# A mixture-of-experts kernel on one core: the first expert weight in two transfers of 4 MB instead of four of 2 MB

## What is computed

```python
def moe_ffn(x, w_router, b_router, w_e1, b_e1, w_e2, b_e2):
    logits = (xt @ w_router + b_router).astype(jnp.float32)
    top_val, top_idx = lax.top_k(logits, TOP_K)      # TOP_K = 4
    gate = jax.nn.softmax(top_val, axis=-1).astype(x.dtype)
    ...
    def expert_block(args):
        xb, e = args
        hb = xb @ w_e1[e] + b_e1[e]
        return clamped_swiglu(hb) @ w_e2[e] + b_e2[e]
```

## Time and profile before

| | us |
|---|---|
| median of 3 runs (1545.33 to 1546.18) | 1546.01 |
| the profiled execution, its own time | 1544.39 |
| its span, first to last instruction | 1542.6 |
| expert loop, about | 600 to 1500 |

### The profile page before, as it was taken

One profiled execution on the slowest core, in us unless ns is written; L12 is line 12 of the kernel. 1 busy time (PEld: TensorE's weight loads), 2 busy tenths in 40 slices (PEclk: granted clock), 3 DMA queues, 4 the chain that ended last, 5 costly groups with the idle time before them and its releaser, 6 DMA issues.

```text
span 1542.6 us, 29979 instructions
## 1 busy us (share of the span) xinstructions
PE 1410.8 (91%) x12414; PEld 715.5 (46%) x12415; DVE 679.6 (44%) x1216; ACT 154.0 (10%) x287; POOL 328.1 (21%) x389
## 2 busy tenths in 40 slices
PE   7999999999999998999986788898789899999987
PEld 6887444458874644443332223333233334444442
DVE  5177344333334764354344334443444334434455
ACT  4112322111110120000000000000000000000001
POOL 1060000000000044233323322332233222323210
PEclk9999999999999999999999999999999999999999
DMA  6533100263317599999999999999999999999997
GB/s 220 188 123 102 28 0 1 53 200 96 95 49 307 202 367 416 420 423 422 422 423 423 420 424 424 422 421 423 424 422 422 425 422 424 423 422 420 423 394 273
DMA packets 98102, 478.52 MB, mean 310 GB/s; under 512 B 14820, under 2 KB 61316, under 8 KB 72968
## 3 DMA queue, kind: packets, MB, share of 16 engines
q1 hardware_dynamic: 84064, 457.68, 73.4%
q0 software_dynamic: 12080, 16.64, 3.0%
q10 hardware_dynamic: 1912, 3.56, 0.6%
HBM read 471.17 MB, written 23.08 MB: 320 GB/s over the span
## 4 chain that ended last, share of the span: by engine, by line
PE 70%; DMA 23%; DVE 3%; issue 2%; another core or an unknown queue 1%; ACT 1%; POOL 0%; SPq 0%; DVEq 0%; POOLq 0%; ACTq 0%
PE ps L1962 23%; DMA big<-in_w_e 22%; PE ps L2007 14%; PE ps L1655 12%; PE ps L1858 4%; PE ps L1822 4%; PE ps L1643 3%; PE ps L1739 2%; PE ps L1788 2%; PE ps L1799 2%; PE ps L1757 1%; PE ps L1806 1%; PE ps L1767 1%; DMA rest<-x_rows,P 1%
## 5 line engine op out<-in xcount | busy, mean ns | idle before, releaser
L1962 PE MATMUL ps<-big,rest 128*32 128x512 f32 x5024 | 557.9, 594 | 73.1 <-DMA big<-in_w_e 53.6
L1962 PEld LDWEIGHTS ps<-big,rest 128*32 128x32 f32 x5024 | 167.2, 110 | 448.7 <-issue 439.4
L2007 PE MATMUL ps<-big,rest 128*32 128x256 f32 x4992 | 292.0, 381 | 29.2 <-DMA big<-in_w_e 23.6
L2007 PEld LDWEIGHTS ps<-big,rest 128*32 128x32 f32 x4992 | 174.4, 110 | 154.5 <-issue 50.3
L1484 DVE MEMSET stat<- 128x1 f32 x30 | 1.8, 59 | 468.9 <-PE ps L1962 468.9
L770 POOL DMA_INDIRECT rest<-x_rows,idx x120 | 147.3, 1228 | 57.2 <-issue 31.7
L786 POOL DMA_INDIRECT expert_rows<-rest,slot x120 | 119.2, 994 | 53.9 <-issue 28.4
L1029 ACT ACTIVATE rest<-rest 128x1024 f32<-128x1024 f32 x32 | 33.9, 1060 | 898.5 <-DVE rest L1463 743.0
L778 POOL COPY idx<-P 128x4 uint32 (+1 forms) x30 | 5.5, 185 | 437.7 <-DVE rest L1485 428.6
L746 POOL IOTA P<- 128x128 f32 x1 | 0.2, 243 | 349.8 <-DVE rest L1311 349.8
L1500 DVE TENSOR_TENSOR rest<-ps,rest 128x1024 f32<-128x1024 f32 x32 | 39.2, 1225 | 66.8 <-PE ps L2007 65.8
(11 more groups left out here) (329 smaller groups left out, 1240.0 us busy)
## 6 DMA issues: line engine op xcount, KB each, us to landing
big<-in_w_e SPq DMA_DIRECT2D x187, 2048.0 KB, 24.3
rest<-in_w_in SPq DMA_DIRECT2D x14, 1024.0 KB, 5.5
big<-expert_rows SPq DMA_DIRECT2D x4, 2048.0 KB, 14.7
gate_area<-in_w_in SPq DMA_DIRECT2D x8, 512.0 KB, 4.8
rest<-in_w_in SPq DMA_DIRECT2D x8, 512.0 KB, 4.8
big<-in_w_out SPq DMA_DIRECT2D x1, 4096.0 KB, 12.8
gate_area<-in_w_e SPq DMA_DIRECT2D x2, 2048.0 KB
X<-in_x SPq DMA_DIRECT2D x4, 512.0 KB, 9.4
```

What stands on the lines that cost most here:

```text
L1962: last = mm(ps[TB * g:TB * (g + 1), h0 + b, :], rows[:, k, b, :], quarter_of(k, g), start=(k == 2 * order[0]), stop=(k == 2 * order[-1] + 1))
L2007: last = mm(ps[TB * g:TB * (g + 1), 4 + b // 2, YW * (b % 2):YW * (b % 2 + 1)], acts[:, k, b, :], rows_of(k, g), start=(first and k == 0), ...
```

## The change

`load_w1` issues two loads instead of four, each for two neighbouring pairs (32 KB in each partition, 4 MB in all), when TensorE has used the second of the two. The landing is counted on the semaphore of the odd pair. In the loop TensorE waits for it ahead of the even pair, and no longer waits ahead of the odd one. The turn that is written out ahead of the loop keeps its waits, since the pairs that it uses still come one by one.

```diff
             def load_w1(it, e):
-                for k in range(PAIRS):
+                for k in range(1, PAIRS, 2):
                     sp.wait_ge(w1_used, PAIRS * it - PAIRS + k + 1)
-                    load_pair(e, k)
+                    sp.dma_start(W1_pairs[:, k - 1:k + 1, :].rearrange("p k n -> p (k n)"), first_rows(e)[:, 4 * FF * (k - 1):4 * FF * (k + 1)]).then_inc(w1_landed[k], 16)
...
             def later_fc1(it1, blocks, pair):
 
-                if pair == SECOND_SPARE:
-                    pe.wait_ge(w1_landed[pair], 16 * it1)
-                else:
-                    pe.wait_ge(w1_landed[pair], 16 * it1 - 16)
+                if isinstance(it1, int):
+                    pe.wait_ge(w1_landed[pair], 16 * it1 if pair == SECOND_SPARE else 16 * it1 - 16)
+                elif pair % 2 == 0:
+                    pe.wait_ge(w1_landed[pair + 1], 16 * it1 - 16)
```

## The result

| | before | after |
|---|---|---|
| median of 6 runs each, us | 1546.01 | 1551.14 |
| lowest to highest, us | 1545.33 to 1546.83 | 1549.69 to 1552.64 |
| ratio, with its 95% interval | 1 | 1.0034 (1.0022 to 1.0047) |
| the profiled execution, us | 1544.39 | 1549.69 |
| its span, us | 1542.6 | 1547.9 |

The change costs 5.1 us (the ratio gives 5.3); 1549.7 was forecast. The profiled executions differ by 5.3 us, so the two traces can be compared for it.

What follows compares the result with a forecast made beforehand. The prediction took one continuous stream of about 174 loads to bound the kernel; 1.7 + 3.3 - 2.8 + 1.5 = +3.7 us on the median 1546.01 gave 1549.7, slower by 0.24%, range 1545.0 to 1555.0.

Steps and rivals of the forecast that it cites:

- (a) Fewer waits and issues: On SyncE, two waits and two loads fewer a turn; worth 0, since SyncE mostly waits for TensorE with the queue full.
- (b) Joint wait: TensorE starts two pairs together; worth 0 with two-block experts, but 5.0 us late relative to the stream from three-block experts on.
- (c) Late issue, first turn: First loop turn: the even pair's load goes out only with the odd one's; the stream loses 1.7 us (0 to 4).
- (c) Four blocks: Expert of four blocks, about 1364 to 1386 us: late joint loads make the stream lose 3.3 us (0 to 6.8).
- (d) Larger packets: All joint loads: 32 KB packets instead of 16 save 6 ns a packet; -2.8 us (0 to -2.8).
- (e) The end: Last expert: pairs 2 and 3 start at one landing, so TensorE ends later beyond the stream's loss; +1.5 us (0 to 1.6).
- The signs: DMA share below 1.01, pauses only near 622 to 635 and 1372 to 1386, first product about 5 us later, 428 to 431 GB/s.
- No cushion: In both tight places the mean engine's pause counts in full, 4 + 6.8; sum +9.5, 1555.5 us; chance 0.10.
- Packets stay at 16 KB: Rows are cut at 16 KB, so joint loads gain nothing from packet size; +6.5, 1552.5 us; chance 0.18.
- Faster: Joint loads hide all pauses behind the late engines, slowest over 5 us behind the mean; 1543.2 us; chance 0.06.
- A fixed cost per transfer: Each load holds the queue for a set time besides its bytes, so 58 fewer would free it; chance 0.01.
- Gathers: Gather packets wait behind 32 KB packets, 7.3 us for a gather of four; if data come late, 1554 us; chance 0.05.

Runs made afterwards that it cites:

- the second trace: The changed kernel timed again on another chip, against the kernel before: 1551.90 us against 1545.89, ratio 1.0037.
- the late issue alone: Kernel before, with the even pair's 2 MB load held back until the odd pair is used; TensorE waits for each pair alone: 1548.39 us, ratio 1.0017.
- both edits: Changed kernel with each 4 MB load as two of 2 MB issued together, in 16 KB packets: 1559.78 us, ratio 1.0081 against the kernel before.
- its control: Kernel before with its loop split in three, all loads single: 1545.93 us, ratio 0.9991; again on another chip 1547.14 us, ratio 1.0004.
- the kernel with joint loads in the early experts: Joint loads for experts 3 to 19 only, single after, loop split, against the kernel before: 1548.29 us, ratio 1.0000.

## Why the prediction was right, step by step

The forecast of +3.7 us had the sign, the two places and the order of size; the median came out 1.4 us above it. That it came so close is in part luck: several terms were off by 1 to 2 us in both directions, and one, the end, had the right number by another path. Step by step:

**(a) Fewer waits and issues, 0.** Nothing in the traces speaks against it.

**(b) Joint wait.** The mechanism held: TensorE starts the three-block expert 4.6 us late, and 5.0 relative to the stream were forecast, at 1257.0 plus what the stream had lost; it came at 1255.75 with the stream 0.1 to 0.3 us early. That pair 1 started at 1257.00 "as it landed" is not in the row, whose 0.52 us of idle time end by "issue"; the last landing of that pair that the trace before has is at 1256.36. The lateness is there at 1353.66 (3.75 us after 1349.91). In the two-block stretch the stream's share is 1.01, so the late waits were swallowed. Not foreseen: they are long enough to lower TensorE's clock (below).

**(c) Late issue, first turn: 1.7 us (0 to 4).** TensorE at 610.59 (610.6 forecast), the first joint load at 621.36 (621.4), the pause of the mean engine 2.3 and 3.7 us in two traces (4.2), the loss of the last 0.8 and 2.3. The size of the term is about right, the path isn't. The forecast had the slowest engine stand 0 us at the first load and 1.6 at the second, issued at 634.0. But every engine stood at the first, for 2.5 us (3.7 in the second trace), and the second went out at 631.61 and met a queue that never ran dry: TensorE did not wait for pairs 2 and 3 (x192 in 20.81 us from 610.59). Within the forecast itself, 35.46 MB at 620 put pair 3 at 620.45 and not at 620.6, and 4.2 MB (9.9 us) from 623.1 last until 633.0 and not 633.4, which would have made the 1.6 a 2.0. The 1 us from issue to first byte, of which the rows showed 0.33, is borne out by the 0.96 to 0.98 us at the two pauses. What failed beyond that is the word cushion: the distance grew back from 0.9 to 2.7 us by 1121, as the late issue alone shows more plainly, and so the last engine then paid what the mean had lost. In the table of after, the mean engine gains 2.4 us from 656 to 1121 and the last loses 0.2.

**(c) Four blocks: 3.3 us (0 to 6.8).** The mean engine lost 5.9 and 5.8 us (6.1 in both by the landing at 1433) against 6.8 forecast, the last lost 4.4 and 4.1. The step that was mis-sized is the 3.5 by which the slowest engine was to be behind: it was 2.4 and 2.2 behind when the pause came. The landings of the trace before had it already: 2.7 at 1371 and 3.1 at 1495, where the forecast had worked out 4.4 from bytes.

**(d) Larger packets: -2.8 (0 to -2.8).** Under-sized, and the bound too narrow. From packets of 1 KB and 16 KB I had worked out 6 ns a packet; the steps next to the case are 8 ns (16 to 32 KB) and 8.5 to 12 (8 to 16 KB). 58 x 8 packets by 8 ns is 3.7 us; the mean engine's gain between 656 and 1121, 30 joint loads, is 2.4 us or 0.08 a load, so 4.6 in all. That the comparison of both edits with and without them gives 7.9 us I can explain only in part: 3.7 are this term, and the longest times without a packet are some 0.1 us longer each, with 0.6 us more at 1378; the rest is not located. The Trainium skill, "DMA: Bandwidth & Descriptors", section "Why small descriptors are slow (HBM only)", has a fixed cost for each packet and says that it is worth joining them only at 256 bytes or below. The first half agrees with these runs, the second doesn't hold for a stream at a share of 1.01: 928 packets an engine of 8 to 16 KB were 7.9 us.

**(e) The end: +1.5 (0 to 1.6).** 4.25 less 2.7 is 1.55; in the second trace 9.06 less 7.5, 1.6. The number is right, the path isn't. Forecast was that TensorE ends the second product of the expert before 1.6 us later than the stream. It ended at 1501.80 (1494.70 and 7.10) against 1498.84 (1495.18 and 3.66), 2.96 later, 0.3 beyond the 2.7 of the stream. The other 1.3 come through VectorE: its gate for the last expert can start only when that expert's whole first product is done, at 1494.95 instead of 1489.06, and it works through to the turn of the activations (L1493), behind which L1500 releases TensorE:

```profile
1494.70 7.10 PE L2007 MATMUL ps<-big,rest 128*32 128x256 f32 x128
1501.35 2.02 DVE L1493 STREAM_TRANSPOSE rest<-rest 128x1024 f32<-128x1024 f32 x1
1503.30 1.18 DVE L1500 TENSOR_TENSOR rest<-ps,rest 128x1024 f32<-128x1024 f32 x1
1504.58 4.17 PE L2007 MATMUL ps<-big,rest 128*32 128x256 f32 x57 [1.78 <-DVE rest L1500]
```

TensorE stood 1.78 us before this row, and 0.49 before. In the second trace of the kernel after the chain of waits runs through VectorE's gate from 1499.75 to 1508.20. The joint wait is still the origin, but what it makes late is VectorE.

**The sum.** Forecast 1.7 + 3.3 - 2.8 + 1.5 = 3.7. By the trace of the last engine: -0.5 to 600, +0.8 first turn, -1.3 to 1371 (the packets' 2.5 to 3.7, less the distance that grew back), +4.4 four blocks, -0.7 to the end, +1.55 and +1.05: 5.3. A smaller cushion (+1.1), a cushion that has to be refilled (some +1.5) and the wait for the experts' rows (+1.05, not the change's) outweigh the larger gain of the packets; this is the account of one trace, with the median 0.2 below it.

**The signs.** The share from 600 to 1500 is 1.00 against 1.01, with the pauses in the two places named (the first, 619.8 to 622.3, a little before the 622 to 635 of the forecast); outside them the traces show no time without a packet. The loads carry 430 GB/s by the median packet of 32 KB (16 engines, 1220 ns, an estimate), in the 428 to 431 that were named, against 427 by that of 16 KB (614 ns).

**The rivals.** *No cushion* (1555.5) is wrong at the time of the pause and nearly right for one early in the loop; the packets' larger gain is why the total still stayed far below it. *Packets stay at 16 KB* is refuted by the count of packets. *Faster* needed a slowest engine 5 us behind the mean; no trace at 1371 has more than 4.5. Still, joint loads from expert 5 on cost nothing that could be told, with one of the two pauses hidden and the other avoided. *A fixed cost per transfer*: 116 more loads of W1 cost 7.9 us, which the packets explain; a large cost per load has no room. (The 2 us that the Trainium skill puts on a DMA are its figure for the path through GpSimd; these loads are issued by SyncE.) *Gathers*: from 600 to 1500 us the idle time of TensorE at the first product is ended by landings of weights (80.3 us) and by issue (10.0), none by rows.

## What to carry to other kernels

Where one transfer stream is the bound, read what an edit does to the queue at its thinnest places: a load that is merged goes out when its last buffer is free, and that costs only there, while the saving in packets is spread evenly over all loads; so merge where the queue is full, if at all (here it brought some 1.5 us with as much uncertainty), and keep small loads where it is short. The distance between the mean and the slowest DMA engine hid a pause only until it had grown back, so count on it near the end of a stream, not at its start, and read it from the landings of a trace. When a sum comes out right, look whether each term came by its own path. Size the cost of a packet from packets next to the ones at issue.

## What the runs showed of the hardware beyond that

**TensorE's clock fell behind the long waits of the joint kernel.** TensorE in time in the kernel after (two-block experts), and the two stretches behind the first wait:

```profile
822.32 9.74 PE L1962 MATMUL ps<-big,rest 128*32 128x512 f32 x64 [6.75 <-DMA big<-in_w_e]
832.57 7.07 PE L1962 MATMUL ps<-big,rest 128*32 128x512 f32 x64 [0.50 <-DMA big<-in_w_e]
...
853.26 9.64 PE L1962 MATMUL ps<-big,rest 128*32 128x512 f32 x64 [6.71 <-DMA big<-in_w_e]
```

```profile
822.00:827.00 5.00, 4.68 (x24) 1.24 (x28) 0.00 (x0) 0.00 (x0) 2.43 (x3) 0.50 1.00 421
827.00:832.00 5.00, 5.00 (x44) 1.21 (x36) 0.00 (x0) 0.00 (x0) 0.00 (x0) 0.92 0.92 385
```

After 6.75 us of idle time the granted clock is 0.50 (1.2 GHz) for the next 5 us and the 64 matmuls take 9.74 instead of 7.07 us; behind the wait of 3.00 us at 1255.75, 192 took 21.04 at the full 2.4 GHz. The same work before had waits of 1.2 to 1.9 us and no such group. Yet the trace before has one shorter wait with a fall behind it, in the first turn, where the granted clock of 636 to 640 us is 0.5 to 0.6, so no length of a wait follows from these rows:

```profile
636.51 3.81 PE L2007 MATMUL ps<-big,rest 128*32 128x256 f32 x36 [2.69 <-issue]
```

The falls behind the long waits are why the mean clock of the loop is 0.97 and TensorE shows 6 us more of work. Here it costs nothing that could be told: at that place the next landing is later still (share 1.01 from 800 to 1250), and the kernel with joint loads for experts 5 to 22 ran at a mean clock of 0.978 and was no slower than its control at 0.996. Of the 76 us that TensorE stood idle from 800 to 1250 us before, it takes about 10. The Trainium skill, "TensorE: Matmul & The Clock Gate", section "Why this matters for your kernels", warns of gaps of idleness between bursts of matmuls that send the clock back to its lower level; this trace agrees.

**The engines of one load are apart.** They finish it up to 8.0 us from first to last (the kernel with joint loads in the early experts, near its end) and as close as 0.6 us after a pause. After a pause the distance of the last from the mean grows by about 0.1 us an expert (0.9 to 2.7 us over 15 experts in the kernel after). Without one it doesn't simply grow: in the trace before it falls from 2.5 at 656 to 1.7 at 1121 and rises again to 3.1 at 1495.
